# The recurrent mixer's decays, roots and gating in another order, its products and scans all on VectorE

## The reference, cut to what matters

```
proj = x @ w_in                       # 1024 -> 2 x 1024
xr, gate = split(proj)
xr = causal_dwconv(xr, conv_w, conv_b)      # 4 taps
r = sigmoid(xr @ w_a + b_a)           # 4 blocks of 256
i = sigmoid(xr @ w_x + b_x)
log_a = -8 * r * softplus(-lam)
a = exp(log_a)
b = sqrt(-expm1(2 * log_a)) * (i * xr)
h[t] = a[t] * h[t-1] + b[t]           # a scan over the 512 tokens
out = (h * gelu(gate)) @ w_out        # 1024 -> 1024
```

## Time and profile before

| | us |
|---|---|
| median of 3 runs | 2458.39 |
| lowest and highest run | 2455.61, 2462.31 |
| the profiled execution's own time | 2459.2 |
| its span | 2457.4 |
| TensorE busy | 2364.1 |
| VectorE busy | 1404.1 |
| ScalarE busy | 1073.5 |
| GpSimd busy | 260.8 |

### The profile page before, as it was taken

One profiled execution on the slowest core, in us unless ns is written; L12 is line 12 of the kernel. 1 busy time (PEld: TensorE's weight loads), 2 busy tenths in 40 slices (PEclk: granted clock), 3 DMA queues, 4 the chain that ended last, 5 costly groups with the idle time before them and its releaser, 6 DMA issues.

```text
span 2457.4 us, 32534 instructions
## 1 busy us (share of the span) xinstructions
PE 2364.1 (96%) x13373; PEld 1968.9 (80%) x13374; DVE 1404.1 (57%) x2133; ACT 1073.5 (44%) x1844; POOL 260.8 (11%) x249
## 2 busy tenths in 40 slices
PE   8999899999999799999999999999999999999997
PEld 6767788888887688888877788888887779788886
DVE  6656564344475764334474577736486545776355
ACT  5645254233266454223265454434244555544341
POOL 0030230000022520000131011101000000011000
PEclk9989999999999899999999999999999999999998
DMA  5210022322222122233221122232221112222221
GB/s 195 86 43 3 26 79 96 101 95 95 94 89 92 60 92 97 95 96 101 86 92 54 58 95 95 97 100 95 86 95 63 42 37 84 96 102 95 94 94 61
DMA packets 59252, 206.32 MB, mean 84 GB/s; under 512 B 6704, under 2 KB 8800, under 8 KB 58976
## 3 DMA queue, kind: packets, MB, share of 16 engines
q1 hardware_dynamic: 58464, 201.35, 24.5%
q0 software_dynamic: 640, 2.89, 0.3%
HBM read 202.07 MB, written 2.10 MB: 83 GB/s over the span
## 4 chain that ended last, share of the span: by engine, by line
PE 43%; DVE 4%; ACT 2%; issue 1%; POOL 0%; DMA 0%; DVEq 0%; POOLq 0%
PE ps L265 12%; PE ps L266 12%; PE ps L267 12%; PE ps L2644 1%; DVE TM L580 1%; PE ps L2673 1%; PE ps L314 1%; PE ps L316 1%; PE ps L315 1%; PE ps L2657 1%; DVE WL L238 0%; DVE X L583 0%; PE ps L809 0%; ACT WH L230 0%; DVE XL L605 0%
## 5 line engine op out<-in xcount | busy, mean ns | idle before, releaser
L265 PE MATMUL ps<-XH,WH 128*128 128x512 f32 (+1 forms) x2216 | 834.0, 376 | 46.5 <-DVE XL L2068 13.5
L266 PE MATMUL ps<-XL,WH 128*128 128x512 f32 (+1 forms) x2216 | 811.8, 366 | 0.0
L267 PE MATMUL ps<-XH,WL 128*128 128x512 f32 (+1 forms) x2216 | 811.2, 366 | 0.0
L238 DVE TENSOR_TENSOR WL<-RAW,WH 128x1024 fp32r<-128x1024 f32 (+1 forms) x382 | 466.5, 1225 | 247.4 <-ACT WH L230 246.4
L265 PEld LDWEIGHTS ps<-XH,WH 128*128 128x128 f32 x2216 | 420.7, 190 | 133.7 <-issue 36.3
L266 PEld LDWEIGHTS ps<-XL,WH 128*128 128x128 f32 x2216 | 421.2, 190 | 69.8 <-issue 5.9
L267 PEld LDWEIGHTS ps<-XH,WL 128*128 128x128 f32 x2216 | 420.5, 190 | 68.1
L230 ACT ACTIVATE WH<-RAW 128x1024 fp32r<-128x1024 f32 (+1 forms) x382 | 391.2, 1036 | 157.9 <-DMA RAW<-in_w 124.3
L265 PE MATMUL ps<-H,WH 128*128 128x512 f32 (+1 forms) x1104 | 401.1, 363 | 2.1 <-ACT AR L1971 2.1
L266 PE MATMUL ps<-H,WH 128*128 128x512 f32 (+1 forms) x1104 | 399.6, 362 | 0.0
L267 PE MATMUL ps<-H,WL 128*128 128x512 f32 (+1 forms) x1104 | 399.4, 362 | 0.0
(11 more groups left out here) (404 smaller groups left out, 2339.9 us busy)
## 6 DMA issues: line engine op xcount, KB each, us to landing
RAW<-in_w SPq DMA_DIRECT2D x128, 512.0 KB, 3.5
RAW<-in_up SPq DMA_DIRECT2D x88, 512.0 KB, 3.5
RAW<-in_dn SPq DMA_DIRECT2D x32, 512.0 KB, 3.4
RAW<-in_hyb SPq DMA_DIRECT2D x23, 512.0 KB, 3.6
RAW<-in_qkv SPq DMA_DIRECT2D x18, 512.0 KB, 3.4
RAW<-in_kvf SPq DMA_DIRECT2D x17, 512.0 KB, 3.5
RAW<-in_rin SPq DMA_DIRECT2D x16, 512.0 KB, 3.4
RAW<-in_dn SPq DMA_DIRECT2D x16, 384.0 KB, 3.0
```

Source lines behind the costliest of these rows:

```text
L238: dve.e.tensor_tensor(WL[:, s, 0:n], RAW[:, s, 0:n], f32(WH[:, s, 0:n]), ALU.subtract).then_inc(*w_lo.at(u))
L265: pe.e.matmul(out, wh, xh, start=first, stop=False)
L266: pe.e.matmul(out, wh, xl, start=False, stop=False)
L267: return pe.e.matmul(out, wl, xh, start=False, stop=last)
```

## The change

ScalarE does the decays 0 to 2 before the first gate copy, the others between copies 0, 1 and 2, all eight roots around gate copy 3, and then Gelus, copies of the gate and high halves as listed. VectorE does all products of root and i * xr, all scans and all gating products; three calls of `split_lo` stand in between. GpSimd keeps only the product i * xr. The high and low halves of what is gated go to H[24..31] and H[8..15] instead of XH and XL, and so the layer norm behind it waits for rin instead of rwo before it writes XH.

```diff
-        READ_BEFORE = {"mlp0": "hwo", "rin": "w1_0", "mlp1": "rwo", "qkv": "w1_1",
+        READ_BEFORE = {"mlp0": "hwo", "rin": "w1_0", "mlp1": "rin", "qkv": "w1_1",
...
-            act.wait_ge(*(done_of(u, v) if READ_BEFORE[stage] in ("hwo", "rwo", "woa") else (unit_done, u)))
+            act.wait_ge(*(done_of(u, v) if READ_BEFORE[stage] in ("hwo", "woa") else (unit_done, u)))
...
-        def mix_out_pe(pe, name, n, nk, ahead=None):
+        def mix_out_pe(pe, name, n, nk, ahead, xh, xl):
             us, banks = UNIT[name], OUT_BANKS[name]
-            run(ahead or beside(pe, us[:3], banks, XHS[:nk], XLS[:nk], ready_of(name, nk)))
+            run(ahead or beside(pe, us[:3], banks, xh, xl, ready_of(name, nk)))
...
-        GATED_ON_POOL = 6
+
+        REC_HI, REC_LO = [H[:, 24 + i, :] for i in range(8)], [H[:, 8 + i, :] for i in range(8)]
...
             def gate(m):
-                split_hi(act, rin[8 + m] + AHEAD)
                 act.wait_ge(unit_done, rin[8 + m])
                 act.e.activation(GA[m], PS[m % 4][:, :], ACT.Copy).then_inc(*ev_act.at(rin[8 + m]))
...
-            for m in range(4):
+            def high(i):
+                act.wait_ge(dve_own, ("gated", i))
+                act.e.activation(REC_HI[i], XR[i], ACT.Copy).then_inc(*x_hi.at(("rwo", i)))
+
+            split_hi(act, rin[8] + AHEAD)
+            for n in range(3):
+                decay(n)
+            for m in range(3):
                 gate(m)
-                decay(2 * m)
-                decay(2 * m + 1)
-            for m in range(4, 8):
-                gate(m)
-                if m < 6:
-                    for n in range(4 * m - 16, 4 * m - 12):
-                        root(n)
-                if m == 6:
-                    for n in range(6):
-                        gated(n)
-            act.wait_ge(unit_done, rin[-1])
-            for i in range(8):
-                act.wait_ge(r_y if i < GATED_ON_POOL else dve_own, ("gated", i))
-                act.e.activation(XH[:, i, :], XR[i], ACT.Copy).then_inc(*x_hi.at(("rwo", i)))
-                if i == 3:
-                    gated(6)
-                    gated(7)
+                split_hi(act, rin[9 + m] + AHEAD)
+                for n in (3 + 2 * m, 4 + 2 * m)[:2 if m < 2 else 1]:
+                    decay(n)
+            split_hi(act, rwo[1])
+            for n in range(4):
+                root(n)
+            gate(3)
+            for n in range(4, 8):
+                root(n)
+            gate(4)
+            split_hi(act, rwo[2])
+            for n in range(5):
+                gated(n)
+            gate(5)
+            split_hi(act, rwo[3])
+            gated(5)
+            high(0)
+            high(1)
+            gate(6)
+            gated(6)
+            for i in range(2, 6):
+                high(i)
+            gate(7)
+            gated(7)
+            high(6)
+            high(7)
...
             def gated(m):
-                if m >= GATED_ON_POOL:
-                    dve.wait_ge(r_g, m)
-                    dve.wait_ge(r_h, m)
-                    dve.e.tensor_tensor(XR[m], XR[m], GA[m], ALU.mult).then_inc(*dve_own.at(("gated", m)))
-
-            for m in range(4):
-                split_lo(dve, rin[8 + m] + AHEAD)
-                decay(2 * m)
-                decay(2 * m + 1)
-            for m in range(4, 8):
-                split_lo(dve, rin[8 + m] + AHEAD)
-                if m < 6:
-                    for n in range(4 * m - 16, 4 * m - 12):
-                        dve.wait_ge(r_y, ("b", n))
-                        dve.e.tensor_tensor_scan(XR[n], RA[n], RB[n], 0.0, ALU.mult, ALU.add).then_inc(*r_h.at(n))
...
+                dve.wait_ge(r_g, m)
+                dve.wait_ge(r_h, m)
+                dve.e.tensor_tensor(XR[m], XR[m], GA[m], ALU.mult).then_inc(*dve_own.at(("gated", m)))
+
+            def scan(n):
+                dve.wait_ge(r_s, n)
+                dve.e.tensor_tensor(RB[n], RB[n], XR[n], ALU.mult).then_inc(*dve_own.at(("b", n)))
+                dve.wait_ge(dve_own, ("b", n))
+                dve.e.tensor_tensor_scan(XR[n], RA[n], RB[n], 0.0, ALU.mult, ALU.add).then_inc(*r_h.at(n))
+
+            def low(m):
+                dve.wait_ge(x_hi, ("rwo", m))
+                dve.e.tensor_tensor(REC_LO[m], XR[m], f32(REC_HI[m]), ALU.subtract).then_inc(*x_lo.at(("rwo", m)))
+
+            split_lo(dve, rin[8] + AHEAD)
+            for n in range(3):
+                decay(n)
+            for m in range(3):
+                split_lo(dve, rin[9 + m] + AHEAD)
+                for n in (3 + 2 * m, 4 + 2 * m)[:2 if m < 2 else 1]:
+                    decay(n)
+            split_lo(dve, rwo[1])
+            for n in range(5):
+                scan(n)
+            split_lo(dve, rwo[2])
+            gated(0)
+            gated(1)
+            scan(5)
+            low(0)
+            low(1)
+            gated(2)
+            gated(3)
+            split_lo(dve, rwo[3])
+            gated(4)
+            gated(5)
+            scan(6)
+            low(2)
+            low(3)
+            scan(7)
+            gated(6)
+            low(4)
+            low(5)
+            gated(7)
+            low(6)
+            low(7)
...
-            for m in range(8):
-                pool.wait_ge(r_s, m)
-                pool.e.tensor_tensor(RB[m], RB[m], XR[m], ALU.mult).then_inc(*r_y.at(("b", m)))
-            for m in range(GATED_ON_POOL):
-                pool.wait_ge(r_g, m)
-                pool.wait_ge(r_h, m)
-                pool.e.tensor_tensor(XR[m], XR[m], GA[m], ALU.mult).then_inc(*r_y.at(("gated", m)))
...
-            mix_out_pe(pe, "rwo", 2, 8)
+            mix_out_pe(pe, "rwo", 2, 8, None, REC_HI, REC_LO)
```

More of the change, by code:

```diff
@@ L832, in mixed @@
             return lambda m, v: (x_mix, (key, *earlier(m, v)))
-        def mix_out_pe(pe, name, n, nk, ahead=None):
+        def mix_out_pe(pe, name, n, nk, ahead, xh, xl):
             us, banks = UNIT[name], OUT_BANKS[name]
-            run(ahead or beside(pe, us[:3], banks, XHS[:nk], XLS[:nk], ready_of(name, nk)))
+            run(ahead or beside(pe, us[:3], banks, xh, xl, ready_of(name, nk)))
             for i in range(4):
                 if i == 3:
-                    unit(pe, us[3], banks[3], XHS[:nk], XLS[:nk], ready_of(name, nk))
+                    unit(pe, us[3], banks[3], xh, xl, ready_of(name, nk))
                 pe.until[banks[i]] = [mixed((name,))(i, None)]
-            last_four_pe(pe, us, XHS[:nk], XLS[:nk], ready_of(name, nk), mixed((name,)), lambda: stats_pe(pe, n, 0, True))
+            last_four_pe(pe, us, xh, xl, ready_of(name, nk), mixed((name,)), lambda: stats_pe(pe, n, 0, True))
         def mix_take_dve(dve, name, x_was):
@@ L1917, in build_program @@
         g_x, g_r, g_i, g_ix = signal("g_x"), signal("g_r"), signal("g_i"), signal("g_ix")
-        r_t, r_a, r_q, r_b, r_s, r_h, r_g, r_y = [signal("r_" + x) for x in ("t", "a", "q", "b", "s", "h", "g", "y")]
-        GATED_ON_POOL = 6
+        r_t, r_a, r_q, r_b, r_s, r_h, r_g = [signal("r_" + x) for x in ("t", "a", "q", "b", "s", "h", "g")]
+        REC_HI, REC_LO = [H[:, 24 + i, :] for i in range(8)], [H[:, 8 + i, :] for i in range(8)]
         def recurrent_pe(pe):
@@ L1950, in recurrent_act @@
         def recurrent_act(act):
-            rin, rwg = UNIT["rin"], UNIT["rwg"]
+            rin, rwg, rwo = UNIT["rin"], UNIT["rwg"], UNIT["rwo"]
             run(softplus_act(act, "lam", NL, COL[:, 8:16], LAM, (gate_dve, "-lam")))
@@ L2971, in tensor_engine @@
             hybrid_in_pe(pe)
-            mix_out_pe(pe, "hwo", 0, 8, hybrid_mix_pe(pe))
+            mix_out_pe(pe, "hwo", 0, 8, hybrid_mix_pe(pe), XHS, XLS)
             mlp_pe(pe, 0)
             recurrent_pe(pe)
-            mix_out_pe(pe, "rwo", 2, 8)
+            mix_out_pe(pe, "rwo", 2, 8, None, REC_HI, REC_LO)
             mlp_pe(pe, 1)
```

## The result

| | median, us | runs | lowest to highest |
|---|---|---|---|
| before | 2458.39 | 5 | 2455.61 to 2462.49 |
| changed | 2439.91 | 5 | 2439.13 to 2447.19 |

The ratio is 0.9927, 95% interval 0.9912 to 0.9942. With the executions of the experiments the kernel before has 73, mean 2460.5, and the changed one 26, mean 2443.8, median 2444.3: 16.7 apart, with a standard error of 0.6 if all executions are taken alike.

What follows compares the result with a forecast made beforehand. TensorE, busy 96% of the span, bounds the kernel; its 13.62 us hole plus 1.68 us of slow clock make 15.30. 2459.2 - 15.3 = 2443.9, on the median 2443.1; forecast 2443.4 us, range 2440.5 to 2450.

Steps and rivals of the forecast that it cites:

- The hole and its cold matmuls, 15.30: Before the recurrent mixer's output product: TensorE's empty 13.62 us plus 1.68 us lost to the lower clock behind it, all removed.
- The walk through ScalarE's and VectorE's queues: Recurrent mixer, instruction by instruction: first root 6.8 us earlier, low halves early by 3.6 us or more, no TensorE wait left.
- the last high half: ScalarE's last high half of the gated values in the recurrent mixer, forecast at 816.8 us.
- the gate copies: ScalarE's copies of the gate units, moved behind other work: forecast to end before TensorE wants their banks, at no cost.
- the split of rwo[3]: VectorE's weight split behind the last high half, forecast to end near 820.3 us with 6 us to spare.
- s = 1.14: Time of one big VectorE scan, start to start, with GpSimd idle; the eight rows of that shape showed 2.18 us.
- B: Rival: big scans keep 2.18 us, TensorE waits in pieces, gain only 9 to 10.8 us (2448.4 to 2450); chance 0.11.
- D: Rival: slower, VectorE's two-input instructions stay at the contended price, 1.68 us for 24 and 2.18 for 8 scans; 2475; chance 0.03.
- Every other stage moves along one for one: Stages outside the changed one: TensorE-bound as before and merely shifted, though small holes elsewhere may meet the clock otherwise.
- Rival C: Hole goes but 2 to 5 us return, through clock falls in later norm stages or a late split; 2445.5 to 2449; chance 0.12.
- A: The forecast case: hole before the output product gone, -15.3 us, for any scan time up to 1.6 us; chance 0.74.
- A by 2 or 3 us to either side for the spread of the runs: How the range was set: the forecast case with that spread, extended up to B's end, giving 2440.5 to 2450 us.

Runs made afterwards that it cites:

- The busy GpSimd: Changed kernel plus 14 products of 128x512 on GpSimd that nobody waits for, VectorE's queue untouched: median 2446.83 us, ratio 0.9947.

## Why the prediction missed by a little

- *The hole and its cold matmuls, 15.30.* Right: the stage took 47.60 in each of five profiles, against 62.9 to 63.0 in four of the kernel before.
- *The walk through ScalarE's and VectorE's queues.* Right within 0.8 us (the last high half, which ended at 816.0 and not at 816.8, is the farthest off), low halves within 0.25; the gate copies released nobody, and the split of rwo[3] was 6.9 us early.
- *s = 1.14.* Right, for the reason given: the row of the 16-partition scan and not the eight of the same shape. The busy GpSimd shows it both ways in one trace. Rivals B and D fall, D with products of 0.66 to 0.69 in the changed kernel.
- *Every other stage moves along one for one.* This put a term at nothing that is not quite nothing. The norm behind the stage gave 1.3 more where its short fall of the clock stayed away, an average of 0.9 over the profiles, and the last 1560 us took 0.3 more on average. Rival C had the place and the wrong sign: it looked for falls gained, not lost. The stage, the norm and the end make 15.3 + 0.9 - 0.3 = 15.9.
- *"A by 2 or 3 us to either side for the spread of the runs".* This is the term that failed. It left 2.9 us below the forecast of 2443.4, and the measured median, 2439.91, lies 3.5 below. The executions of one and the same kernel spread over 9 us (2439.1 to 2448.0 for the changed one), and the part ahead of the second gate copy alone over 5.5 us (776.9 to 782.4). The five that set the measured median held three of the five lowest of all 26: 2439.13, 2439.30 and 2439.91. 26 executions have their median at 2444.3, 0.9 above the forecast, and a gain by means of 16.7. So over all of them the forecast stands in its range. That the first five left it is for the most part luck of which executions came, but perhaps not all: the five below 2440 were all among the first ten of the changed kernel, and none among the 16 that followed.
- *What made those executions short stays open.* None of the five was profiled. Their mean granted clock was 0.992 to 0.994, that of the others 0.990 to 0.993. The shortest parts seen in any profile of the changed kernel add up to 776.9 + 47.6 + 55.35 + 1560.4 = 2440.2, and the span of the execution of 2439.13 was 2437.3. So it saved 2.9 us that no trace of this kernel shows.

## What to carry to other kernels

Before a duration is taken from a row, see what the neighbour engine did in that row: eight rows at 2.2 us said less on the scan's cost than one of another shape taken beside an idle GpSimd. A long wait that ends on the last of a chain is emptied by walking each engine's queue from the first instruction that can move, and enabling parts (a buffer that is free earlier) show nothing alone and 6.8 us together with the rest. And a forecast of a half-percent gain needs the spread of single executions in its range, more than the uncertainty of its mechanism.

## What had not been expected of the hardware

- A short fall of the clock need not repeat from one execution to the next: of 16 profiles, with the change, without it and with parts of it, TensorE fell to its lower level in the same norm in eleven and kept the higher one in five. Before and changed kernel have the same wait of 2.55 us ahead of it. It makes 1.3 us.
- The matmuls behind an empty slot can lose more when the slot is shorter: 3.0 us behind 4.7, 2.6 behind 9.0, 1.7 behind 13.6, but also 1.7 behind 2.0, each from one kernel's trace. In the three longer ones the granted clock rose again 5.8, 5.3 and 3.2 us after the matmuls had begun, and half of that is about the loss.
- Products of one constant with itself on GpSimd held VectorE up by 0.75 us an instruction, products of two different tiles by 1.0. How long they hold it up may depend on what GpSimd reads. It may also depend on the spacing, since each of the first kind also waited by semaphore for the one before it; neither was tried by itself.
